# A hybrid decoder step on one core: x loaded in whole rows by token tile, and the first projection begun with half of the tokens

## The chip, the core and the metric

The kernel runs on one core of one Trainium2 chip. The metric is the device time of one execution in microseconds, the median of repeated runs. The engines named below are TensorE (PE in the profile; its weight loads are PEld), VectorE (DVE), ScalarE (ACT), GpSimd (POOL) and SyncE (SP), which issues most of the DMA transfers. Each engine works through its own instructions in their order and stops at a wait until a semaphore has reached a value.

## The reference, cut to what matters

One layer of a decoder over 512 prompt tokens and 8 x 4 sample tokens, 544 in all, with 1024 channels in float32. Only the first lines bear on the change:

```python
def token_mixer(x, w_in, w_out, lb, ...):
    proj = x @ w_in                       # 544 x 1024 @ 1024 x 3584
    q, fz, i, g, gb, gc, cx = jnp.split(proj, ...)
    ...                                   # HGRN2 recurrence, short gated convolution
    return jnp.concatenate([o, yc], axis=-1) @ w_out, S_new, new_buf

def trunk(x, ...):
    m, S_l, b_l = token_mixer(x, ...)
    x = layer_norm(ALPHA * x + m, ln1_g, ln1_b)
    x = layer_norm(ALPHA * x + grouped_moe(x, w_router, ...), ln2_g, ln2_b)
```

Every part that follows (the recurrence, the output projection, the router, 16 experts of width 512) needs the projection, and so does the end of the kernel.

## The kernel before, in words

**Arithmetic.** A float32 matrix product is made of three products of rounded parts: each operand is split into a part `hi` (a copy in the type fp32r) and a rest `lo` (the operand minus `hi`), and hi*hi, hi*lo and lo*hi are added up in one PSUM bank. ACT writes every `hi`, DVE every `lo`, which needs `hi` first.

**Stages.** First the front, on which the change bears: x arrives, is turned (transposed) by PE, split by ACT and DVE, and the first weights are split. Then 14 chunks of the input projection of 256 columns each (`project_first` for chunk 0, `project(o)` for the others), with the gates, the recurrence and the convolution worked in between; the output projection; layer norm and routing; the experts; the final sum. The order on each engine is written out by hand; no scheduler changes it.

**The front before.** There are five token tiles: four of 128 tokens and one of 32. `xT` holds x turned, channels on the partitions, 544 tokens in the free dimension, for each of 8 channel tiles `kt`. The work goes by halves of the channels, `hf` 0 and 1:

- SP (L441 to L447) issues for a half the 512 columns of each of the five token tiles (rows of 2 KB, 256 KB for a tile of 128 tokens), and then half of the weights of chunk 0 (`w0`, rows of 1 KB, 512 KB). After both halves comes chunk 1 of the weights (1 MB), then constants, masks and parameters, chunk 2, and each later chunk when its buffer is free: chunk c waits for `s_lo` at c - 2, since there are three buffers.
- PE (`turn_x`, L1444) waits for a tile's half, turns it in four transposes into one PSUM bank and goes on to the next tile; there are ten such groups, m = 0 to 9, of which m = 4 and 9 are the tile of 32 tokens. Groups 8 and 9 use banks 3 and 4 a second time.
- ACT (L693) copies each turned group from PSUM into `xT[0]` as `hi`, and DVE (L966) writes `lo` into `xT[1]`. Between the two halves ACT and DVE split the first half of `w0` (L703, L977); after the second half of x they split the second half of `w0` (L713, L983 with 1024 columns), then chunk 1 (the same lines with 2048).
- PE then runs `project_first` (L1461): chunk 0 has two tiles of 128 output columns, n = 0 and 1. For each kt and each of the three products it loads one piece of weights for tokens 0 to 271 (L1477) and once more for tokens 272 to 543 (L1478), into two banks; HT is 272. It takes channel tiles 0 to 3 for both n, waits for the second half of the weights, and takes 4 to 7. That is 96 matmuls of 272 tokens.
- `project(1)` (L1504, L1505) needs chunk 1 split (`s_lo` at 2) and the bank of tile 0 emptied by ACT.
- POOL waits for all ten groups of x and for `s_lo` at 2 and then writes 4 MB of zeros to a buffer in DRAM (L574).

Of the kernel before, what the change touches and what calls it, by code (L numbers as in the profile page):

```python
# [34 lines left out]
P = 128  # L35
D = 1024
KT = D // P
SEQ, DB, DS = 512, 8, 4
NS = DB * DS
T = SEQ + NS  # L40
# [75 lines left out]
def build(nc, a):  # L116
    ctx = ExitStack()

    def sem(name):
        return ctx.enter_context(nc.semaphore(name))  # L120

    with ctx:
# [101 lines left out]
        s_x = [sem(f"x_in{i}") for i in range(2 * NTT)]  # L224
# [82 lines left out]
        def x_bank(m):  # L307

            return (0, 1, 2, 3, 4, 5, 6, 7, 3, 4)[m]

        def x_place(m):

            n = P if m % NTT < 4 else NS
            c0 = P if m == 2 * NTT - 1 else 0
            return bank[x_bank(m)][:, c0:c0 + 4 * n]
# [110 lines left out]
        def _(sp):  # L426
# [14 lines left out]
            for hf in range(2):  # L441
                cols, ks = slice(512 * hf, 512 * hf + 512), slice(4 * hf, 4 * hf + 4)
                for tt in range(4):
                    sp.dma_start(xn[:, tt, cols], a["x_prompt"][0, tt * P:(tt + 1) * P, cols]).then_inc(s_x[NTT * hf + tt], 16)
                sp.dma_start(xn[0:NS, 4, cols], a["x_sample"].rearrange("b t n -> (b t) n")[:, cols]).then_inc(s_x[NTT * hf + 4], 16)
                sp.dma_start(raw[0].rearrange("p (k n) -> p k n", k=KT)[:, ks, :], w0[:, ks, :]).then_inc(
                    s_w0 if hf == 0 else s_raw[0], 16)  # L447
# [235 lines left out]
        def _(act):  # L683
# [9 lines left out]
            def x_hi_front(hf):  # L693
                for tt in range(NTT):
                    m = NTT * hf + tt
                    n = P if tt < 4 else NS
                    act.wait_ge(s_xt, m + 1)
                    src = x_place(m).rearrange("p (k t) -> p k t", k=4)
                    nc.scalar.activation(xT[0][:, 4 * hf:4 * hf + 4, tok(tt)], src, ACT.Copy).then_inc(s_xh, 1)

            x_hi_front(0)
            act.wait_ge(s_w0, 16)
            nc.scalar.activation(split[0][0][:, 0:1024], raw[0][:, 0:1024], ACT.Copy).then_inc(s_h0, 1)  # L703
            x_hi_front(1)
# [40 lines left out]
            for o in range(NCH + 1):  # L745
# [5 lines left out]
                hi(o)  # L751
                if o == 4:
                    act.wait_ge(s_abs, 1)
                    link(nc.scalar.activation(ex[0][:, :, :], ex[0][:, :, :], ACT.Exp, scale=-1.0))
                    nc.scalar.activation(ex[0][:, :, :], ex[0][:, :, :], ACT.Ln, bias=1.0).then_inc(s_lnf, 1)
# [197 lines left out]
        def _(dve):  # L953
# [12 lines left out]
            def x_lo_front(hf):  # L966
                for tt in range(NTT):
                    m = NTT * hf + tt
                    n = P if tt < 4 else NS
# [5 lines left out]
            x_lo_front(0)  # L975
            dve.wait_ge(s_h0, 1)
            tt_(split[0][1][:, 0:1024], raw[0][:, 0:1024], f(split[0][0][:, 0:1024]), ALU.subtract).then_inc(s_l0, 1)  # L977
            x_lo_front(1)
# [74 lines left out]
            for o_ in range(NCH + 1):  # L1053
# [5 lines left out]
                lo(o_)  # L1059
                if o_ == 1:  # L1060
                    dve.wait_ge(s_const, 16)
                    dve.wait_ge(s_mask, 16)
                    link(nc.vector.tensor_copy(masks[:, :], fa(E0, LEVELS * P)))
# [378 lines left out]
        def _(pe):  # L1442
            mm, tr = nc.tensor.matmul, nc.tensor.transpose
            def turn_x(hf):  # L1444
                for tt in range(NTT):
                    m = NTT * hf + tt
                    rows = P if tt < 4 else NS
                    pe.wait_ge(s_x[m], 16)
                    if m >= 8:
                        pe.wait_ge(s_xl, m - 4)  # L1450
                    for j in range(4):
                        kt = 4 * hf + j
                        last = tr(x_place(m)[:, j * rows:(j + 1) * rows], xn[0:rows, tt, kt * P:(kt + 1) * P],
                                  ident[0:rows, 0:rows])
                    last.then_inc(s_xt, 1)

            pe.wait_ge(s_id, 16)
            turn_x(0)
            turn_x(1)

            def project_first():  # L1461

                wh, wl = chunk_weights(0, 0), chunk_weights(0, 1)
                pe.wait_ge(s_xl, NTT)
                pe.wait_ge(s_l0, 1)
                for hf in range(2):
                    if hf:
                        pe.wait_ge(s_lo, 1)
                    for n in range(2):
                        if n == 1 and hf == 0:  # L1470
                            pe.wait_ge(s_xl, 2 * NTT)
                        pb, ps = tile_banks(n)
                        for kt in range(4 * hf, 4 * hf + 4):
                            for i, (w_, x_) in enumerate(((wh, 0), (wh, 1), (wl, 0))):
# [433 lines left out]
```

## Time and profile before

| what | us |
|---|---|
| median of 3 runs (lowest, highest) | 698.58 (697.02, 699.57) |
| the profiled execution's own time | 699.09 |
| its span, first to last instruction | 697.3 |
| PE busy | 663.2 (95%) |
| DVE busy | 505.2 (72%) |
| ACT busy | 344.4 (49%) |
| POOL busy | 134.8 (19%) |

The granted TensorE clock is 0.976 of full speed over the span. PE is busy nearly all of the time. Times in the rows count from the start of the span; 1.8 us of the profiled execution's time lie outside the span. The page cuts the span into 40 slices of 17.4 us, so the whole front lies in the first and in half of the second.

### The profile page before, as it was taken

To read this page: it belongs to the slowest core of one execution; us is meant where nothing else is said; L and a number is where in the kernel's file an instruction comes from. 1 tells how busy PE (TensorE), PEld (TensorE's weight loads), DVE (VectorE), ACT (ScalarE), POOL (GpSimd) and SP (SyncE) were. 2 spreads that over 40 slices of the span, in tenths; PEclk is the share of its full clock that TensorE was granted. 3 is DMA by queue.
4 is the path that set the end of the run, shared out by engine and by line. 5 is a ranking of instruction groups with operands and counts; after the bars stand their busy time and mean duration, and the time that the engine had idled before them with its cause. 6 is when DMAs were issued, how large, how long until landed. Compare 5 with 4: busy or idle time off the path is not lost. (4 is left out here: it accounts for less than half of the span.)

```text
span 697.3 us, 9659 instructions
## 1 busy us (share of the span) xinstructions
PE 663.2 (95%) x3847; PEld 559.2 (80%) x3847; DVE 505.2 (72%) x579; ACT 344.4 (49%) x339; POOL 134.8 (19%) x81
## 2 busy tenths in 40 slices
PE   6999999988999999999979999999999999999786
PEld 5999899988997897577857888888888888888531
DVE  4226336798766384758684999999999999999626
ACT  4537412222226141111505777777777777777402
POOL 0001414422131220400020011111111111100055
PEclk9999999999999999999898999999999999999998
DMA  8951111211612105069346999999999999994164
GB/s 285 381 198 62 61 61 62 69 53 61 190 53 85 53 16 193 0 185 410 138 160 274 328 417 419 397 415 409 407 415 411 404 413 406 410 404 173 47 242 158
DMA packets 48689, 162.56 MB, mean 233 GB/s; under 512 B 4294, under 2 KB 23450, under 8 KB 36364
## 3 DMA queue, kind: packets, MB, share of 16 engines
q1 hardware_dynamic: 41756, 136.62, 51.4%
q0 software_dynamic: 6896, 25.43, 9.3%
q8 instruction: 25, 0.41, 0.2%
q14 instruction: 12, 0.10, 0.0%
HBM read 142.61 MB, written 19.44 MB: 232 GB/s over the span
## 5 line engine op out<-in xcount | busy, mean ns | idle before, releaser
L1322 DVE TENSOR_TENSOR RA<-FA,RA 128x2048 fp32r<-128x2048 f32 x93 | 212.9, 2290 | 29.4 <-ACT RA L859 28.7
L859 ACT ACTIVATE RA<-FA 128x2048 fp32r<-128x2048 f32 x93 | 178.9, 1924 | 46.3 <-PE bank L1777 30.6
L1777 PE MATMUL bank<-RA 128*128 128x512 f32 x768 | 186.9, 399 | 2.7 <-DVE RA L1327 2.6
L1777 PEld LDWEIGHTS bank<-RA 128*128 128x128 f32 x768 | 142.9, 191 | 34.6 <-DVE RA L1327 3.5
L1504 PE MATMUL bank<-RA 128*128 128x272 f32 x432 | 110.3, 292 | 0.0
L1505 PE MATMUL bank<-RA 128*128 128x272 f32 x432 | 109.6, 290 | 0.0
L1789 PE MATMUL bank<-RA 128*128 128x512 f32 x384 | 89.9, 390 | 1.4 <-DVE RA L1332 1.4
L1789 PEld LDWEIGHTS bank<-RA 128*128 128x128 f32 x384 | 72.0, 188 | 16.5 <-DVE RA L1332 1.6
L1504 PEld LDWEIGHTS bank<-RA 128*128 128x128 f32 x432 | 82.5, 191 | 0.0
L1505 PEld LDWEIGHTS bank<-RA 128*128 128x128 f32 x432 | 82.3, 191 | 0.0
L983 DVE TENSOR_TENSOR RA<-FA,RA 128x2048 fp32r<-128x2048 f32 (+1 forms) x18 | 48.6, 2700 | 27.3 <-ACT RA L713 27.0
L713 ACT ACTIVATE RA<-FA 128x2048 fp32r<-128x2048 f32 (+1 forms) x18 | 33.6, 1867 | 58.1 <-PE bank L1505 27.5
L1497 PE MATMUL bank<-RA 128*128 128x256 f32 (+1 forms) x480 | 58.8, 282 | 2.0 <-ACT FA L725 2.0
L1497 PEld LDWEIGHTS bank<-RA 128*128 128x128 f32 (+1 forms) x480 | 56.1, 172 | 4.7 <-ACT FA L725 2.4
L629 POOL DMA_INDIRECT FA<-x_by_token,ids x16 | 39.7, 2483 | 79.8 <-DVE ids L1299 60.2
L646 POOL DMA_DIRECT2D y_by_slot<-FA x16 | 9.1, 571 | 236.5 <-DVE FA L1339 236.5
L1659 PE MATMUL bank<-RA 128*128 128x512 f32 x192 | 48.3, 408 | 0.0
L1659 PEld LDWEIGHTS bank<-RA 128*128 128x128 f32 x192 | 36.7, 194 | 10.9 <-issue 2.5
L584 POOL TENSOR_TENSOR FA<-FA 128x1024 f32<-128x1024 f32 (+1 forms) x7 | 16.6, 2365 | 113.5 <-PE bank L1539 69.3
L760 ACT ACTIVATE FA<-FA 128x2048 f32<-128x2048 f32 (+1 forms) x7 | 13.6, 1947 | 49.7 <-POOL FA L585 49.7
L1042 DVE COPY_PREDICATED FA<-masks,bank 128x512 f32<-128x512 uint8 x28 | 20.1, 734 | 22.3 <-PE bank L1539 21.9
L1539 PE MATMUL bank<-FA 128*128 128x128 f32 x256 | 31.0, 278 | 3.9 <-DVE FA L1042 3.9
(237 smaller groups left out, 774.1 us busy)
## 6 DMA issues: line engine op xcount, KB each, us to landing
FA<-w_up SPq DMA_DIRECT2D x32, 1024.0 KB, 7.6
FA<-w_gate SPq DMA_DIRECT2D x32, 1024.0 KB, 7.3
FA<-w_down SPq DMA_DIRECT2D x32, 1024.0 KB, 7.8
FA<-w_in SPq DMA_DIRECT2D x13, 1024.0 KB, 4.9
y_by_slot<-FA POOLq DMA_DIRECT2D x16, 512.0 KB, 7.5
y_by_slot<-FA POOLq DMA_DIRECT2D x1, 4096.0 KB, 18.1
FA<-w_out SPq DMA_DIRECT2D x4, 1024.0 KB, 5.0
FA<-x_prompt SPq DMA_DIRECT2D x8, 256.0 KB, 5.4
```

Source lines behind the costliest of these rows:

```text
L629: pool.indirect_dma_start(out=xg[par], out_offset=None, in_=x1_dram, in_offset=bass.IndirectOffsetOnAxis(ap=ids[:, bi:bi + 1].bitcast(U32) ...
L713: nc.scalar.activation(split[o % 2][0][:, cs], raw[o % 3][:, cs], ACT.Copy).then_inc(s_hi, 1)
L859: nc.scalar.activation(split[split_slot(bi, j)][0], raw[place], ACT.Copy).then_inc(m_hi, 1)
L983: tt_(split[o % 2][1][:, cs], raw[o % 3][:, cs], f(split[o % 2][0][:, cs]), ALU.subtract).then_inc(s_lo, 1)
L1322: tt_(sl[1], raw[place], f(sl[0]), ALU.subtract).then_inc(m_lo, 1)
L1497: last = mm(pb[0:rows, 0:CW], xT[x_][:, kt, tok(j)], w_[:, kt, :], start=(kt == 0 and i == 0), stop=(kt == KT - 1 and i == 2))
L1504: mm(pb[:, 0:HT], lhs, xT[x_][:, kt, 0:HT], start=first, stop=end)
L1505: last = mm(ps[:, 0:HT], lhs, xT[x_][:, kt, HT:T], start=first, stop=end)
L1539: last = mm(bank[4 + p % 3][:, cols], lf[:, h, cols], rf[:, h, cols], start=True, stop=True)
L1659: last = mm(w_bank(half, tt)[0:rows, :], xT[x_][:, k0 + kt, tok(tt)], w_[:, kt, :], start=(conv and kt == 0 and i == 0), stop=(not conv an ...
L1777: last = mm(out[:, :], xgT[par][x_][:, kt, :], w[w_][:, t, :], start=(kt == 0 and i == 0), stop=(kt == KT - 1 and i == 2))
L1789: last = mm(bank[5 + g][:, :], hT[x_][:, kt, :], w[w_][:, t, 512 * g:512 * g + 512], start=(kt == 0 and i == 0), stop=(kt == 3 and i == 2))
```

## The change

x is loaded in whole rows of 4 KB, one transfer for each token tile. The three first tiles come first, then the two halves of `w0`, then tiles 3 and 4. `turn_x(tt)` turns both halves of a tile after one wait. Before the projection PE turns tiles 0 to 2 alone. The projection of chunk 0 is then cut by tokens and no longer by channels: part 0 makes tokens 0 to 271 for n = 0 and n = 1, all eight channel tiles, and part 1 makes tokens 272 to 543 for both. Tile 3 is turned after part 0 of n = 0, tile 4 after part 0 of n = 1. ACT and DVE split tiles 3 and 4 after the second half of `w0` and before chunk 1. The PSUM banks of the turned groups are dealt out anew. The numbers of matmuls, transposes and splits stay.

```diff
         def x_bank(m):
-            return (0, 1, 2, 3, 4, 5, 6, 7, 3, 4)[m]
+            return (4, 5, 6, 7, 2, 3, 4, 5, 6, 7)[m]
...
             w0 = w_in[:, :, ORDER[0][1] * CW:(ORDER[0][1] + 1) * CW]
-            for hf in range(2):
-                cols, ks = slice(512 * hf, 512 * hf + 512), slice(4 * hf, 4 * hf + 4)
-                for tt in range(4):
-                    sp.dma_start(xn[:, tt, cols], a["x_prompt"][0, tt * P:(tt + 1) * P, cols]).then_inc(s_x[NTT * hf + tt], 16)
-                sp.dma_start(xn[0:NS, 4, cols], a["x_sample"].rearrange("b t n -> (b t) n")[:, cols]).then_inc(s_x[NTT * hf + 4], 16)
-                sp.dma_start(raw[0].rearrange("p (k n) -> p k n", k=KT)[:, ks, :], w0[:, ks, :]).then_inc(
-                    s_w0 if hf == 0 else s_raw[0], 16)
+            for tt in range(3):
+                sp.dma_start(xn[:, tt, :], a["x_prompt"][0, tt * P:(tt + 1) * P, :]).then_inc(s_x[tt], 16)
+            for ks, signal in ((slice(0, 4), s_w0), (slice(4, 8), s_raw[0])):
+                sp.dma_start(raw[0].rearrange("p (k n) -> p k n", k=KT)[:, ks, :], w0[:, ks, :]).then_inc(signal, 16)
+            sp.dma_start(xn[:, 3, :], a["x_prompt"][0, 3 * P:4 * P, :]).then_inc(s_x[3], 16)
+            sp.dma_start(xn[0:NS, 4, :], a["x_sample"].rearrange("b t n -> (b t) n")).then_inc(s_x[4], 16)
             load_w(1)
...
-            x_hi_front(0)
+            for tt in range(3):
+                x_hi_front(tt)
             act.wait_ge(s_w0, 16)
             nc.scalar.activation(split[0][0][:, 0:1024], raw[0][:, 0:1024], ACT.Copy).then_inc(s_h0, 1)
-            x_hi_front(1)
...
                 hi(o)
+                if o == 0:
+                    x_hi_front(3)
+                    x_hi_front(4)
...
                 lo(o_)
+                if o_ == 0:
+                    x_lo_front(3)
+                    x_lo_front(4)
...
             pe.wait_ge(s_id, 16)
-            turn_x(0)
-            turn_x(1)
+            for tt in range(3):
+                turn_x(tt)
 
             def project_first():
 
                 wh, wl = chunk_weights(0, 0), chunk_weights(0, 1)
-                pe.wait_ge(s_xl, NTT)
+                pe.wait_ge(s_xl, 6)
                 pe.wait_ge(s_l0, 1)
-                for hf in range(2):
-                    if hf:
-                        pe.wait_ge(s_lo, 1)
+                for part, cols in enumerate((slice(0, HT), slice(HT, T))):
+                    if part:
+                        pe.wait_ge(s_xl, 2 * NTT)
                     for n in range(2):
-                        if n == 1 and hf == 0:
-                            pe.wait_ge(s_xl, 2 * NTT)
-                        pb, ps = tile_banks(n)
-                        for kt in range(4 * hf, 4 * hf + 4):
+                        to = tile_banks(n)[part]
+                        for kt in range(KT):
+                            if n == 0 and kt == 4 and part == 0:
+                                pe.wait_ge(s_lo, 1)
                             for i, (w_, x_) in enumerate(((wh, 0), (wh, 1), (wl, 0))):
-                                first, end = kt == 0 and i == 0, kt == KT - 1 and i == 2
-                                lhs = w_[:, kt, n * P:(n + 1) * P]
-                                mm(pb[:, 0:HT], lhs, xT[x_][:, kt, 0:HT], start=first, stop=end)
-                                last = mm(ps[:, 0:HT], lhs, xT[x_][:, kt, HT:T], start=first, stop=end)
-                        if hf:
+                                last = mm(to[:, 0:HT], w_[:, kt, n * P:(n + 1) * P], xT[x_][:, kt, cols],
+                                          start=(kt == 0 and i == 0), stop=(kt == KT - 1 and i == 2))
+                        if part:
                             last.then_inc(s_tile, 1)
+                        else:
+                            turn_x(3 + n)
```

On PE before, from the last groups turned to the first matmuls of the projection (L1453 are transposes, L1477 and L1478 matmuls; `x_in8` is the semaphore of one tile's half, `xT_lo` counts the groups split by DVE):

```order
L1453 MATMUL bank3<-FA 128x128 [waits xT_lo,x_in8]
L1453 MATMUL bank3<-FA 128x128 x3
L1453 MATMUL bank4<-FA 128x32 [waits xT_lo,x_in9]
L1453 MATMUL bank4<-FA 128x32 x3
L1477 MATMUL bank0<-RA 128x272 [waits lo_first_half,xT_lo]
L1478 MATMUL bank2<-RA 128x272
```

On PE after the change, from tile 2 of x to the start of chunk 1 (L1452 are transposes, L1474 the matmuls of chunk 0):

```order
L1452 MATMUL bank2<-FA 128x128 [waits x_in2]
L1452 MATMUL bank2<-FA 128x128 x3
L1452 MATMUL bank3<-FA 128x128 x4
L1474 MATMUL bank0<-RA 128x272 [waits lo_first_half,xT_lo]
L1474 MATMUL bank0<-RA 128x272 x11
L1474 MATMUL bank0<-RA 128x272 [waits lo_done]
L1474 MATMUL bank0<-RA 128x272 x11
L1452 MATMUL bank4<-FA 128x128 [waits x_in3]
...
L1474 MATMUL bank1<-RA 128x272 x24
L1452 MATMUL bank6<-FA 128x32 [waits x_in4]
...
L1474 MATMUL bank2<-RA 128x272 [waits xT_lo]
L1474 MATMUL bank2<-RA 128x272 x23
```

Eight transposes of 128 tokens and eight of 32, which stood ahead of the projection, now stand in it, and the second half of the matmuls has a wait of its own for `xT_lo`.

On SP before, the first transfers (in const_f32 the identity, then x, the halves of w0, and chunk 1):

```order
L427 DMA FA<-const_f32 128x128
L444 DMA FA<-x_prompt 128x512 x4
L445 DMA FA<-x_sample 32x512
L446 DMA FA<-w_in 128x4x256
L444 DMA FA<-x_prompt 128x512 x4
L445 DMA FA<-x_sample 32x512
L446 DMA FA<-w_in 128x4x256
L438 DMA FA<-w_in 128x8x256
```

On SP after the change, the same stretch:

```order
L425 DMA FA<-const_f32 128x128
L440 DMA FA<-x_prompt 128x1024 x3
L442 DMA FA<-w_in 128x4x256 x2
L443 DMA FA<-x_prompt 128x1024
L444 DMA FA<-x_sample 32x1024
L436 DMA FA<-w_in 128x8x256
```

Ahead of the first half of w0 there are now 1536 KB of x where there were 1088 KB; ahead of the second half 1536 KB where there were 2176 KB.

On ACT after the change, from the last of tile 2 to chunk 1 (L695 splits x, L700 and L709 weights; `raw_in0` and `raw_in1` are the transfers of the second half of w0 and of chunk 1):

```order
L695 ACTIVATE RA<-bank3 128x4x128 [waits x_transposed]
L700 ACTIVATE RA<-FA 128x1024 [waits w0_first_half_in]
L709 ACTIVATE RA<-FA 128x1024 [waits raw_in0]
L695 ACTIVATE RA<-bank4 128x4x128 [waits x_transposed]
L695 ACTIVATE RA<-bank5 128x4x128 [waits x_transposed]
L695 ACTIVATE RA<-bank6 128x4x32 [waits x_transposed]
L695 ACTIVATE RA<-bank7 128x4x32 [waits x_transposed]
L709 ACTIVATE RA<-FA 128x2048 [waits raw_in1]
```

The split of chunk 1 now stands behind the last group of x, which PE turns in the middle of its projection; DVE has the same order.

## Rows read from the trace of the kernel before

**Rows 1.** The page's busy times, the engine with the largest share.

```profile
PE 663.2 (95%) x3847; PEld 559.2 (80%) x3847; DVE 505.2 (72%) x579; ACT 344.4 (49%) x339; POOL 134.8 (19%) x81
```

**Rows 2.** Busy time in stretches: stretch, length, busy of each engine, clock, DMA share, GB/s.

```profile
core 0: us, PE busy (x) PEld busy (x) DVE busy (x) ACT busy (x) POOL busy (x), PEclk, DMA share, GB/s
14.59:26.80 12.21, 12.21 (x99) 12.21 (x98) 4.94 (x5) 5.91 (x9) 1.10 (x1) 1.00 1.08 360
26.80:60.00 33.20, 33.20 (x267) 33.20 (x266) 9.21 (x4) 18.30 (x25) 0.00 (x0) 1.00 0.63 234
```

**Rows 3.** What PE waited for over the span: us in total, times, longest.

```profile
PE bank L1453 <- DMA FA<-x_prompt: 6.5, 3, 4.0
PE bank L1497 <- ACT FA L725: 2.0, 2, 1.6
```

**Rows 4.** Timeline of PE, 3 to 15 us: start, length, engine, line, what, count.

```profile
3.98 1.09 PE L1453 MATMUL bank<-FA 128*128 128x128 f32 x4 [3.98 <-DMA FA<-x_prompt]
5.60 2.97 PE L1453 MATMUL bank<-FA 128*128 128x128 f32 x16 [0.54 <-DMA FA<-x_prompt]
10.53 4.13 PE L1453 MATMUL bank<-FA 128*128 128x128 f32 x20 [1.96 <-DMA FA<-x_prompt]
14.59 0.42 PE L1477 MATMUL bank<-RA 128*128 128x272 f32 x1
```

**Rows 5.** Two DMAs, tile 3's first half and w0's second: issue, time to landing.

```profile
L444 SPq DMA_DIRECT2D FA<-x_prompt x1: 432/432/432, 2.6 to 2.6; - x1
DMA to landing us min/median/max: 4.3/4.3/4.3
...
L446 SPq DMA_DIRECT2D FA<-w_in x1: 425/425/425, 6.7 to 6.7; - x1
DMA to landing us min/median/max: 7.8/7.8/7.8
```

**Rows 6.** Timelines of ACT and DVE in the front, the splits of weights.

```profile
9.85 1.06 ACT L703 ACTIVATE RA<-FA 128x1024 fp32r<-128x1024 f32 x1 [0.84 <-DMA FA<-w_in]
17.48 1.92 ACT L713 ACTIVATE RA<-FA 128x2048 fp32r<-128x2048 f32 x1 [1.56 <-DMA FA<-w_in]
...
10.94 1.23 DVE L977 TENSOR_TENSOR RA<-FA,RA 128x1024 fp32r<-128x1024 f32 x1 [1.17 <-ACT RA L703]
19.44 2.29 DVE L983 TENSOR_TENSOR RA<-FA,RA 128x2048 fp32r<-128x2048 f32 x1 [2.25 <-ACT RA L713]
```

**Rows 7.** Splits of x by form, 4 to 15.9 us: busy us, mean ns of one.

```profile
L699 ACT ACTIVATE RA<-bank 128x512 fp32r<-128x512 f32 x8 | 4.8, 597 | 5.9 <-PE bank L1453 5.8
L699 ACT ACTIVATE RA<-bank 128x128 fp32r<-128x128 f32 x2 | 0.5, 274 | 0.0
...
L972 DVE TENSOR_TENSOR RA<-bank,RA 128x128 fp32r<-128x128 f32 x2 | 0.6, 281 | 0.0
```

**Rows 8.** Busy time in three shorter stretches of the front; columns as in rows 2.

```profile
7.90:8.60 0.70, 0.67 (x7) 0.39 (x5) 0.54 (x2) 0.66 (x2) 0.00 (x0) 1.00 0.93 278
...
10.50:11.20 0.70, 0.67 (x5) 0.44 (x5) 0.26 (x1) 0.41 (x1) 0.00 (x0) 1.00 1.04 397
11.30:14.60 3.30, 3.30 (x17) 2.49 (x17) 2.85 (x4) 2.18 (x4) 0.00 (x0) 0.50 1.10 334
```

**Rows 9.** Transposes: two short pieces of the timeline, and the line's durations.

```profile
5.87 1.27 PE L1453 MATMUL bank<-FA 128*128 128x128 f32 x5
...
10.53 0.66 PE L1453 MATMUL bank<-FA 128*128 128x128 f32 x4 [1.96 <-DMA FA<-x_prompt]
...
L1453 PE MATMUL bank<-FA x40: 221/421/476, 4.0 to 14.4; 128*128 128x128 f32 x32, 32*128 32x32 f32 x8
14.03 0.50 PEld L1453 LDWEIGHTS bank<-FA 32*128 32x128 f32 x4 [0.33 <-issue]
```

**Rows 10.** SP's transfer of chunk 4 of the weights: issue, time to landing.

```profile
L438 SPq DMA_DIRECT2D FA<-w_in x1: 368/368/368, 21.8 to 21.8; - x1
DMA to landing us min/median/max: 14.7/14.7/14.7
```

**Rows 11.** The page's group of token-major matmuls, 24 in a row into one bank.

```profile
L1497 PE MATMUL bank<-RA 128*128 128x256 f32 (+1 forms) x480 | 58.8, 282 | 2.0 <-ACT FA L725 2.0
```

More of the change, by code:

```diff
@@ L223, in build @@
         s_const, s_mask, s_par, s_s0 = sem("const_in"), sem("mask_in"), sem("param_in"), sem("s0_in")
-        s_x = [sem(f"x_in{i}") for i in range(2 * NTT)]
+        s_x = [sem(f"x_in{i}") for i in range(NTT)]
         s_raw = [sem(f"raw_in{i}") for i in range(3)]
@@ L307, in x_bank @@
         def x_bank(m):
-            return (0, 1, 2, 3, 4, 5, 6, 7, 3, 4)[m]
+            return (4, 5, 6, 7, 2, 3, 4, 5, 6, 7)[m]
         def x_place(m):
-            n = P if m % NTT < 4 else NS
-            c0 = P if m == 2 * NTT - 1 else 0
-            return bank[x_bank(m)][:, c0:c0 + 4 * n]
+            return bank[x_bank(m)][:, 0:4 * (P if m < 8 else NS)]
         def sum_banks(tt):
@@ L690, in link, with x_hi_front @@
                 act.wait_ge(s_ac, chain[0])
[L693 to L696, printed above, removed]
+            def x_hi_front(tt):
+                for hf in range(2):
+                    m = 2 * tt + hf
                     act.wait_ge(s_xt, m + 1)
@@ L965, in _, with x_lo_front @@
             link(nc.vector.memset(eps_ln, LN_EPS))
[L966 to L969, printed above, removed]
+            def x_lo_front(tt):
+                for hf in range(2):
+                    m = 2 * tt + hf
                     dve.wait_ge(s_xh, m + 1)
@@ L973, in x_lo_front @@
                         ALU.subtract).then_inc(s_xl, 1)
-            x_lo_front(0)
+            for tt in range(3):
+                x_lo_front(tt)
             dve.wait_ge(s_h0, 1)
             tt_(split[0][1][:, 0:1024], raw[0][:, 0:1024], f(split[0][0][:, 0:1024]), ALU.subtract).then_inc(s_l0, 1)
-            x_lo_front(1)
             def lo(o):
@@ L1443, in _, with turn_x @@
             mm, tr = nc.tensor.matmul, nc.tensor.transpose
[L1444 to L1450, printed above, removed]
+            def turn_x(tt):
+                rows = P if tt < 4 else NS
+                pe.wait_ge(s_x[tt], 16)
+                for hf in range(2):
+                    m = 2 * tt + hf
                     for j in range(4):
@@ L1457, in _ @@
             pe.wait_ge(s_id, 16)
-            turn_x(0)
-            turn_x(1)
+            for tt in range(3):
+                turn_x(tt)
             def project_first():
                 wh, wl = chunk_weights(0, 0), chunk_weights(0, 1)
-                pe.wait_ge(s_xl, NTT)
+                pe.wait_ge(s_xl, 6)
                 pe.wait_ge(s_l0, 1)
-                for hf in range(2):
-                    if hf:
-                        pe.wait_ge(s_lo, 1)
+                for part, cols in enumerate((slice(0, HT), slice(HT, T))):
+                    if part:
+                        pe.wait_ge(s_xl, 2 * NTT)
                     for n in range(2):
-                        if n == 1 and hf == 0:
-                            pe.wait_ge(s_xl, 2 * NTT)
-                        pb, ps = tile_banks(n)
-                        for kt in range(4 * hf, 4 * hf + 4):
+                        to = tile_banks(n)[part]
+                        for kt in range(KT):
+                            if n == 0 and kt == 4 and part == 0:
+                                pe.wait_ge(s_lo, 1)
                             for i, (w_, x_) in enumerate(((wh, 0), (wh, 1), (wl, 0))):
-                                first, end = kt == 0 and i == 0, kt == KT - 1 and i == 2
-                                lhs = w_[:, kt, n * P:(n + 1) * P]
-                                mm(pb[:, 0:HT], lhs, xT[x_][:, kt, 0:HT], start=first, stop=end)
-                                last = mm(ps[:, 0:HT], lhs, xT[x_][:, kt, HT:T], start=first, stop=end)
-                        if hf:
+                                last = mm(to[:, 0:HT], w_[:, kt, n * P:(n + 1) * P], xT[x_][:, kt, cols],
+                                          start=(kt == 0 and i == 0), stop=(kt == KT - 1 and i == 2))
+                        if part:
                             last.then_inc(s_tile, 1)
+                        else:
+                            turn_x(3 + n)
                 pe.wait_ge(s_par, 64)
```

## The prediction

> **What bounds the kernel now.** I read the page's busy times first: PE is busy 95% of the span [rows 1]. Then the busy times by stretch, from the start: from the first matmul of the projection at 14.59 us PE is busy for 12.21 of 12.21 us, and on to 60 us for 33.20 of 33.20 [rows 2]. Then what PE waited for: 6.5 us on transfers of x, and of all later waits the first (2.0 us, on ACT) comes in a stretch whose work is itself released by earlier projection tiles [rows 3]. The reader is to see that behind 14.59 us PE holds everything else. A shift of the end of chunk 0, which now ends as chunk 1 starts at about 26.8, therefore goes one for one into the total, both ways. The question is only when chunk 0 ends.
>
> The timeline of PE in the front [rows 4] shows what comes ahead of it: transposes at 3.98, from 5.60 to 8.57, a gap of 1.96 us, and transposes again from 10.53 to 14.66, as the second halves of x land. In the window 7.9 to 8.6 and again at 10.5 to 11.2 the granted clock is 1.00, but from 11.3 to 14.6, after the gap, it is 0.50 (the level of 1.2 GHz); it is 1.00 again in the projection [rows 8, 2]. So before the change the slow stretch falls upon transposes that wait for data anyway, and the 96 matmuls run at full clock.
>
> **When the projection starts.** The new start needs tile 2 of x turned and split, and the first half of w0 split. I place transfers by the KB ahead of them in the queue, the identity's 64 KB counted.
>
> Before, tile 3's first half (1088 KB with all ahead) was there at 2.6 + 4.3 = 6.9, the first half of w0 (1664 KB) at 9.85, where ACT's wait ended, and the second half of w0 (3264 KB) at 6.7 + 7.8 = 14.5 [rows 5, 6]. That is 195 KB/us from 6.9 to 9.85, and 344 KB/us after that. Tile 0 whole (576 KB) is there at 5.6, where PE's second wait ended with the same bytes moved [rows 4]. Tile 1 (1088 KB) follows at 6.9. Tile 2 (1600 KB) lands between 6.9 + 512/344 = 8.4 and 6.9 + 512/195 = 9.5; I take 9.0. The first half of w0 (2112 KB) lands between 9.9 (8.4 + 1.5) and 9.85 + 448/344 = 11.15; I take 10.6.
>
> A transpose takes a slot of (1.27 - 0.42)/4 = 0.21 us at the start, where 0.42 is the median of one, and at most (0.66 - 0.22)/3 = 0.15 later, when the clock is full, where 0.22 is the shortest; half of 0.21 is the lower bound there [rows 9]. Eight cost 1.7, or 0.9 to 1.2. PE turns tile 0 from 5.6 to 7.3, tile 1 to about 8.6, tile 2 from 9.0 to 10.0, its last result at 10.3. ACT copies the last group, 0.60 [rows 7], to 10.9. Then the first half of w0: 1.06 on ACT to 12.0, 1.23 on DVE [rows 6] to 13.3 with the handovers. The projection starts at 13.3, that is 1.3 us sooner than at 14.59. Bounds: with the early landings 12.6 (2.0 sooner); with the late ones and tile 2 turned at the slow spacing 14.4 (0.2 sooner).
>
> **What the projection now carries.** Its 96 matmuls stay. That 24 in a row go to one bank costs nothing that the trace shows: the token-major tiles do so at 58.8/480 = 0.12 us each [rows 11], and 12.21/99 is 0.12 too [rows 2].
>
> - Tile 3 turned inside: 8 transposes at full clock, 0.9 to 1.2, at most 1.7: I take 1.0. Its transfer (3136 KB) lands at about 14.1 by the same rates, before PE comes to it behind 24 matmuls (3.0 us), so no wait.
> - Tile 4 turned inside: four such loads took 0.50 [rows 9] at the slow clock, so eight cost 0.5 to 1.0: 0.5.
> - The wait for `xT_lo` ahead of part 1. Nothing lies between PE's last transpose and it, so PE stands still for the end of that transpose (0.2 to 0.3), ACT 0.27, DVE 0.28 [rows 7] and three handovers: 0.85, bounds 0.7 to 1.0. Everything is queued behind it, part 1 of both tiles.
> - The wait for the second half of w0 in the middle of the first 24 matmuls costs nothing: it lands near 12.6, ACT is free for it at 12.0 and done at 13.7, DVE takes 1.23 more, to 14.9; PE comes there at 13.3 + 1.5 = 14.8 at full clock, later at half.
> - The clock. PE idles from 10.3 to 13.3, 3.0 us; before, a gap of 1.96 was followed by 3.3 us at 0.50 with PE busy throughout [rows 8]. That stretch now falls on matmuls. 3.3 us at half clock do 1.65 us of work. I take 1.7 lost; from both sides, 0 (the clock stays) and 2.4 (a slow stretch longer by as much as the gap is, half as long again: 3.3 x 1.5 / 2).
>
> The work behind chunk 0 has cover. ACT and DVE split chunk 1 only after tile 4: 1.92 and 2.29 us [rows 6], some 4.1 from the point where part 1 starts, and part 1 runs for 48 slots, 6.0. PE stays covered by 1.9 us; without that cover the rest of it would be paid. Chunk 4 of the weights, whose transfer waits for that split, is issued some 6 us later than 21.8, took 14.7 to land beside POOL's write of zeros [rows 10], and is split only after 50 us, so it stays hidden too. SP issues 11 transfers where it issued 13.
>
> Sum: -1.3 + 1.0 + 0.5 + 0.85 + 1.7 = +2.75 us. The end of chunk 0 goes from 26.8 to about 29.5. The profiled execution's 699.09 would be 701.8; it stands 0.5 above the median of the runs, 698.58, so the median is predicted at 701.3. Ends of the sum: -2.0 + 0.9 + 0.5 + 0.7 + 0 = +0.1 and -0.2 + 1.7 + 1.0 + 1.0 + 2.4 = +5.9.
>
> A rule against part of this. The clock was 1.00 at 7.9 to 8.6 and at 10.5 to 11.2, when PE had run nothing but transposes [rows 8]. The Trainium skill, TensorE: Matmul & The Clock Gate, section Part 4: PE-mode transpose, says that the full clock does not engage for transposes, which do not count as a busy PE in the same way. By that rule tile 2 would be turned at the slow spacing; the trace disagrees, since the spacing of transposes also shrank there.
>
> **The rivals.**
>
> 1. The clock stays full. For it: transposes up to 10.3 leave less room for a gap ahead of a drop; the start may come earlier. Against: the gap is half as long again as the one that a drop followed. Then +1.05: 699.6.
> 2. The transfers bring no earlier start. Whole rows put 448 KB more ahead of the first half of w0, and ACT and DVE must split all of tile 2 ahead of it. For it: the slow 195 KB/us at just this point in the queue. Start at 14.4, tile 3 at 1.0, clock 2.0: -0.2 + 1.0 + 0.5 + 0.85 + 2.0 = +4.2, with the slow spacing +5: 703.2.
> 3. The other side: faster. The start moves by more than the projection takes on. It decides at 1.0 + 0.5 + 0.85 = 2.35 us with the clock full, so at a start before 12.2. That needs tile 2 by 8.0 and the first half of w0 by 9.8, as if rows of 4 KB moved at 400 KB/us and more. A start at 11.4 gives -0.85: 697.7. Against: 344 KB/us is the rate shown, and the split of the weights alone takes 2.3 us behind the last copy.
> 4. Transposes never raise the clock. Tile 2 then costs 0.7 more ahead of the start and nothing else changes, as matmuls run before tile 3: +3.45: 702.0. The spacing of rows 9 speaks against it. It is the result of the skill's rule above.
>
> **How the numbers follow.** The forecast has 0.45, rival 1 0.23, rival 2 0.19, rival 3 0.07, rival 4 0.04; 0.02 is for what I don't see. A measurement of this kernel can tell about 0.5% from no change, here 3.5 us: slower means above 702.1, faster below 695.1. Slower takes most of rival 2 (0.16), half of rival 4 and a third of the forecast, whose own range is 699.8 to 703.2: 0.34. Faster is out of reach of rival 3 (it would need a start before 9, ahead of the first half of w0), so 0.04 for all else. The rest is 0.62. The ends of the sum put the median at 698.7 to 704.5; the runs of the kernel before spread by 1.3 to either side. With most of rival 3 left out at the bottom the range is 697.7 to 705.0.
>
> **What would show it.** In the profile after: the first L1474 starts at 12.6 to 14.4; the clock is 0.50 for some 3 us that overlap it; the matmuls of chunk 0 fall into four blocks with L1452 between them; PE waits once for DVE, 0.7 to 1.0 us, ahead of part 1; L1503 starts at 28.5 to 31; no new wait ahead of L1503. It is wrong if the start is before 12.2, if L1503 waits for the split of chunk 1, or if later stages do not keep the shift.

## The result, and the profile after

| | before | changed |
|---|---|---|
| median (lowest, highest), 14 runs each | 699.09 (695.50, 700.79) | 700.95 (698.15, 703.56) |
| ratio to the kernel before, 95% interval | | 1.0031 [1.0017, 1.0045] |
| profiled execution, span | 699.09, 697.3 | 698.15, 696.3 |
| mean granted clock of the profiled execution | 0.976 | 0.977 |
| first matmul of chunk 0 / chunk 1 | 14.59 / 26.79 | 12.58 / 28.48 |

The change costs 1.9 us in the median, 0.3%: clear of the interval, but under the 0.5% that was called a difference. The profiled execution of the changed kernel happens to be a fast one, faster than that of before. So the times are compared by the medians, and the profile is read where it is sharp: at the two ends of chunk 0.

The timeline of PE from 4 to 12.7 us, which answers to [rows 4], in two rows of transposes and the first matmul:

```profile
4.49 3.65 PE L1452 MATMUL bank<-FA 128*128 128x128 f32 x16 [4.49 <-DMA FA<-x_prompt]
8.30 1.25 PE L1452 MATMUL bank<-FA 128*128 128x128 f32 x8 [0.16 <-DMA FA<-x_prompt]
12.58 0.56 PE L1474 MATMUL bank<-RA 128*128 128x272 f32 x1 [3.03 <-DVE RA L976]
```

The last transpose of tile 2 ends at 9.55, and PE stands for 3.03 us until DVE has made `lo` of the weights. Pieces of the same timeline further on, one for each block change:

```profile
16.99 1.04 PE L1452 MATMUL bank<-FA 128*128 128x128 f32 x8
17.78 0.37 PE L1474 MATMUL bank<-RA 128*128 128x272 f32 x1
...
20.97 0.68 PE L1452 MATMUL bank<-FA 32*128 32x32 f32 x8
22.34 0.39 PE L1474 MATMUL bank<-RA 128*128 128x272 f32 x1 [0.69 <-DVE RA L970]
...
28.45 0.24 PE L1481 MATMUL bank<-FA 84*128 84x84 f32 x1
28.48 0.37 PE L1503 MATMUL bank<-RA 128*128 128x272 f32 x1
```

The start moved by -2.01, chunk 1 by +1.69; chunk 0 takes 15.90 us instead of 12.20. The busy times of the changed kernel by stretch, which answer to [rows 2, 8]:

```profile
core 0: us, PE busy (x) PEld busy (x) DVE busy (x) ACT busy (x) POOL busy (x), PEclk, DMA share, GB/s
28.45:60.00 31.55, 31.55 (x254) 31.55 (x253) 9.21 (x4) 16.62 (x25) 0.00 (x0) 1.00 0.63 233
8.70:9.50 0.80, 0.80 (x8) 0.61 (x6) 0.69 (x1) 0.43 (x2) 0.00 (x0) 1.00 1.12 393
9.60:12.10 2.50, 0.00 (x0) 0.00 (x0) 2.18 (x3) 2.27 (x4) 0.00 (x0) 1.00 1.07 310
12.20:15.40 3.20, 2.82 (x12) 2.85 (x13) 1.46 (x2) 0.26 (x1) 0.00 (x0) 0.50 1.10 325
```

From 12.2 to 15.4 the clock is 0.50, and now it lies on the first matmuls: 12 of them in 2.82 us. After chunk 1 has started PE is busy all the time again. ACT and DVE around the weights (timelines, answering to [rows 6]):

```profile
9.15 1.08 ACT L695 ACTIVATE RA<-bank 128x512 fp32r<-128x512 f32 x2 [0.37 <-PE bank L1452]
10.12 1.06 ACT L700 ACTIVATE RA<-FA 128x1024 fp32r<-128x1024 f32 x1
21.85 1.91 ACT L709 ACTIVATE RA<-FA 128x2048 fp32r<-128x2048 f32 x1
...
11.21 1.23 DVE L976 TENSOR_TENSOR RA<-FA,RA 128x1024 fp32r<-128x1024 f32 x1
23.79 2.29 DVE L981 TENSOR_TENSOR RA<-FA,RA 128x2048 fp32r<-128x2048 f32 x1 [1.51 <-ACT RA L709]
```

ACT goes from the copies of tile 2 to the weights without a wait, so the transfer of the weights, which had landed at 9.8, was not what the start waited for. Chunk 1 is split by 26.1, 2.4 us ahead of its first matmul, more than the 1.9 us of cover that the prediction worked out.

### The profile page after: what moved, and what is told of

Same layout as the page of the kernel before. It is cut to its first block and busy times, and to the rows that moved or that the text cites. A ratio compares the mean times of both kernels' runs of the same rounds, so it can differ in the third digit from the quotient of the medians.

```text
span 696.3 us, 9652 instructions
## 1 busy us (share of the span) xinstructions
PE 662.1 (95%) x3847; PEld 558.1 (80%) x3847; DVE 505.1 (73%) x579; ACT 344.1 (49%) x339; POOL 134.8 (19%) x81
## 5 line engine op out<-in xcount | busy, mean ns | idle before, releaser
L1323 DVE TENSOR_TENSOR RA<-FA,RA 128x2048 fp32r<-128x2048 f32 x93 | 212.9, 2290 | 28.5 <-ACT RA L858 27.8
L1503 PE MATMUL bank<-RA 128*128 128x272 f32 x432 | 109.1, 289 | 0.0
L1504 PE MATMUL bank<-RA 128*128 128x272 f32 x432 | 108.5, 288 | 0.0
L709 ACT ACTIVATE RA<-FA 128x2048 fp32r<-128x2048 f32 (+1 forms) x18 | 33.6, 1867 | 54.0 <-PE bank L1504 26.3
L1658 PEld LDWEIGHTS bank<-RA 128*128 128x128 f32 x192 | 35.5, 188 | 10.5 <-issue 2.5
```

The costliest lines, as they stand in the source:

```text
L709: nc.scalar.activation(split[o % 2][0][:, cs], raw[o % 3][:, cs], ACT.Copy).then_inc(s_hi, 1)
L1323: tt_(sl[1], raw[place], f(sl[0]), ALU.subtract).then_inc(m_lo, 1)
L1658: last = mm(w_bank(half, tt)[0:rows, :], xT[x_][:, k0 + kt, tok(tt)], w_[:, kt, :], start=(conv and kt == 0 and i == 0), stop=(not conv an ...
```

## The experiments

Chunk 1's start and the landings come from one profile for each kernel, the ratios from comparisons with the kernel before on the same chip (10 to 12 executions of the kernel tried).

**The clock: fill the gap.** The changed kernel with matmuls whose result is not used:

```diff
             for tt in range(3):
                 turn_x(tt)
+            pe.wait_ge(s_xh, 3)
+            for _ in range(20):
+                mm(bank[0][:, 0:256], xT[0][:, 0, 0:P], xT[0][:, 1, 0:256], start=True, stop=True)
```

> The changed kernel with 20 matmuls of 256 columns on data that is already there, into bank 0 that the projection clears, put in PE's idle gap ahead of the projection (3.0 us in the changed kernel's profile); their result is not used. Theory A (the slow clock is a term of its own, about 1.5 us, and is caused by that gap): the clock stays 1.00 from about 8.7 on, the projection starts at 12.6 as it did, and chunk 1 begins at 27.0 instead of 28.5; the time is 1.5 us under the changed kernel's, within 0.1% of the kernel before. Rival B (the extra time comes from the new order of the matmuls themselves, 24 in a row into one bank): chunk 1 still begins at 28.5 or later, and the time does not fall.

Ratio 0.9994 [0.9978, 1.0010]. In the timeline of PE and the busy times of this kernel:

```profile
9.89 2.96 PE L1461 MATMUL bank<-RA 128*128 128x256 f32 x20
13.22 0.36 PE L1477 MATMUL bank<-RA 128*128 128x272 f32 x1 [0.37 <-DVE RA L976]
27.81 0.37 PE L1506 MATMUL bank<-RA 128*128 128x272 f32 x1
...
13.30:27.70 14.40, 13.71 (x112) 13.45 (x113) 5.57 (x7) 6.07 (x10) 1.09 (x1) 1.00 0.85 283
```

The clock is 1.00 all through chunk 0, which takes 14.59 us (27.81 - 13.22) instead of 15.90: the slow stretch cost 1.3. Rival B, the order of the matmuls, fails. Chunk 1 begins at 27.8 and not at 27.0, since tile 0 landed later in this execution (PE began at 4.88, not 4.49) and the clock first rose at 10.7, when the unused matmuls already ran (8.7 in the changed kernel), so that tile 2 was turned at the slow spacing; the start is again 2.99 us behind the last transpose, at 10.23. It is the length of chunk 0 that a single profile can tell, not the place of its start.

**The wait: turn tile 4 with tile 3.**

```diff
-                        else:
-                            turn_x(3 + n)
+                        elif n == 0:
+                            turn_x(3)
+                            turn_x(4)
```

> The changed kernel with tile 4 turned right behind tile 3, after part 0 of n = 0; part 0 of n = 1 then stands between the last transpose and the wait of part 1. Theory A (the wait ahead of part 1 costs its 0.7 us because nothing lies between): no wait there any more, chunk 1 begins 0.7 us earlier, at 27.8, with the clock as in the changed kernel. x_sample landed at 14.1 and PE comes to it at about 17.5, so no new wait. Rival: PE waits the same 0.7 elsewhere (for ACT or DVE, for the transfer of tile 4, or for chunk 1, whose split would now be further ahead), and chunk 1 begins at 28.5.

Ratio 1.0008 [0.9991, 1.0025]. What PE waited for from 12 to 60 us, first in this kernel, then in the changed one:

```profile
PE bank L1474 <- DVE RA L976: 3.0, 1, 3.0
```

```profile
PE bank L1474 <- DVE RA L976: 3.0, 1, 3.0
PE bank L1474 <- DVE RA L970: 0.7, 1, 0.7
```

The wait of 0.7 is gone and none has come in its place. Chunk 0 runs from 13.00 to 28.21, 15.21 us: 0.69 less than 15.90. The length of chunk 0 fell as theory A has it, and the rival fails. Chunk 1 itself began at 28.2 and not at 27.8, for a start that was 0.42 later in this execution.

**Turn everything first.** All five tiles ahead of the projection, the loads and the cut by tokens kept:

```diff
-            for tt in range(3):
+            for tt in range(NTT):
+                if tt == 3:
+                    pe.wait_ge(s_xl, 4)
                 turn_x(tt)
...
                         if part:
                             last.then_inc(s_tile, 1)
-                        else:
-                            turn_x(3 + n)
```

> The changed kernel with all five tiles turned ahead of the projection; loads and the cut by tokens stay as in the changed kernel. Theory A (turning inside the projection gives back what the early start brings): the start waits for x_sample, which landed at 14.1, and comes at 14.6 to 15.0; nothing is turned inside and nothing waits, so chunk 1 begins at 26.9 to 27.3 if the clock is full, up to 28.5 if the slow stretch falls on the matmuls. Rival B (the cut by tokens is what costs): the 96 matmuls take over 12.5 us at full clock. Rival C (the early start is worth its whole 2.0 us): chunk 1 begins 2 us later than in the changed kernel, at 30.5.

Ratio 1.0035 [1.0015, 1.0055]. The busy times of this kernel, and the timeline's first matmuls of chunks 0 and 1:

```profile
12.40:15.10 2.70, 2.70 (x16) 2.37 (x16) 2.04 (x4) 1.40 (x3) 0.00 (x0) 0.50 1.12 355
15.20:19.10 3.90, 3.90 (x18) 3.90 (x18) 2.26 (x4) 2.19 (x2) 0.00 (x0) 0.50 1.03 372
19.30:29.00 9.70, 9.70 (x80) 9.70 (x79) 1.18 (x2) 2.66 (x5) 1.09 (x1) 1.00 1.08 371
...
15.18 0.59 PE L1476 MATMUL bank<-RA 128*128 128x272 f32 x1
29.14 0.37 PE L1503 MATMUL bank<-RA 128*128 128x272 f32 x1
```

The start came near the place given (15.2 for 14.6 to 15.0), but not for the reason given: x_sample landed at 12.9 in this execution and not at 14.1, and PE turned without a further wait from 12.33 on, tile 3 at the slow spacing of 0.21 us. The end was missed: 29.1 lies beyond the 28.5 given. The slow stretch was twice as long, from 12.4 to 19.2, and four microseconds of it lay on matmuls. Without it the matmuls take what they took before: 80 in 9.70 us is 0.12 each, so rival B, a cost of the cut by tokens, fails here too. Rival C expected chunk 1 at 30.5 and fails by 1.4. Whether turning early or late is better does not come out clean. With the clock's cost on the matmuls taken off (2.0 of 13.96 us) this order would have ended chunk 0 at 27.1, the changed kernel (1.3 off) at 27.2; but here the slow stretch lay on the transposes ahead of the start too, and tiles 3 and 4 had landed over 1 us sooner. The ratios, 1.0035 and 1.0031, show no gain of the early start over waiting for all of x, and do not decide theory A either.

**Both edits together.**

> The changed kernel with both edits: the 20 unused matmuls in the gap, and tile 4 turned with tile 3. If the terms add (theory A): chunk 1 begins at 28.5 - 1.5 - 0.7 = 26.3, 0.5 us ahead of the kernel before, a time 0.1% under it, which this measurement hardly tells from no change. If they overlap (the rival), it begins at 27.0 as with the matmuls in the gap alone.

Ratio 0.9991 [0.9970, 1.0012]. Chunk 0 from 12.84 to 26.71:

```profile
26.71 0.37 PE L1507 MATMUL bank<-RA 128*128 128x272 f32 x1
12.90:26.60 13.70, 13.70 (x112) 13.49 (x113) 5.50 (x7) 5.88 (x10) 1.09 (x1) 1.00 1.09 352
```

13.87 us: less by 2.03 than 15.90, and 1.31 + 0.69 is 2.00. The terms add. The clock had risen at 8.9, ahead of the gap, and stayed at 1.00, so this is also the cleaner proof that the filled gap keeps it. The end is 26.7, not 26.3, for the start, 0.26 later, and a slow stretch that was worth 1.3 and not 1.5.

**The kernel before, its gap filled.** The same idea in the kernel before, 14 matmuls between the halves of x:

```diff
             turn_x(0)
+            pe.wait_ge(s_xl, 2)
+            for _ in range(14):
+                mm(bank[0][:, 0:256], xT[0][:, 0, 0:P], xT[0][:, 1, 0:256], start=True, stop=True)
             turn_x(1)
```

> The kernel before with 14 unused matmuls of 256 columns in its own gap (8.6 to 10.5 us), ahead of the second halves of x. Theory A (the clock falls because of the gap, in the kernel before too, where the slow stretch hits only transposes that wait for data one by one): the clock stays 1.00, the last tile is turned at 13.6 to 13.9 instead of 14.6, chunk 1 begins 0.6 to 1.0 us earlier than at 26.8. Rival (the transposes there are bound by the transfers): chunk 1 begins at 26.6 to 26.8, no change.

Ratio 0.9966 [0.9945, 0.9986]. Timeline and busy times:

```profile
8.56 1.93 PE L1461 MATMUL bank<-RA 128*128 128x256 f32 x14
10.33 1.36 PE L1453 MATMUL bank<-FA 128*128 128x128 f32 x8
11.95 1.75 PE L1453 MATMUL bank<-FA 128*128 128x128 f32 x12 [0.26 <-DMA FA<-x_prompt]
13.62 0.39 PE L1480 MATMUL bank<-RA 128*128 128x272 f32 x1
25.78 0.37 PE L1507 MATMUL bank<-RA 128*128 128x272 f32 x1
...
10.50:13.60 3.10, 2.71 (x20) 1.81 (x19) 2.53 (x4) 2.03 (x4) 0.00 (x0) 1.00 1.09 344
```

The stretch behind the gap, at 0.50 in [rows 8], has the clock at 1.00. The projection starts 0.97 sooner and chunk 1 1.01 sooner; the second halves of x landed 0.1 to 0.3 sooner in this execution, which can be a part of it. So the gap caused the slow stretch in the kernel before as well, and it was not free there: the prediction called it hidden behind the transfers, and 0.7 us (the last run below, where the transfers were no earlier than before) to 1 us of it was not.

**Rows of 2 KB again.** The changed kernel, tiles 0 to 2 each by two transfers (and `turn_x` waits for both):

```diff
             for tt in range(3):
-                sp.dma_start(xn[:, tt, :], a["x_prompt"][0, tt * P:(tt + 1) * P, :]).then_inc(s_x[tt], 16)
+                for hc in (slice(0, 512), slice(512, 1024)):
+                    sp.dma_start(xn[:, tt, hc], a["x_prompt"][0, tt * P:(tt + 1) * P, hc]).then_inc(s_x[tt], 16)
```

> The changed kernel with each of the tiles 0 to 2 of x loaded by two transfers of rows of 2 KB (256 KB each) instead of one of 4 KB rows, in the same order. In the changed kernel tile 0 landed at 4.4, tile 2 at 8.25 and the first half of w0 at 9.8, all earlier than predicted from the kernel before (5.6, 9.0, 10.6). If whole rows are what makes the transfers faster: tile 0 lands at 5.2 or later, w0's first half at 10.5 or later and the projection starts 0.5 us or more after 12.6. If not (the order alone, or the variation from run to run, in which w0's first half landed between 9.0 and 10.0 in four profiles): tile 0 at 4.4 to 4.9, w0's first half at 9.0 to 10.0, and the start still 3.0 us behind the last transpose of tile 2.

One profile. First the issue and landing of tile 1's second half and of w0's first half, then the timeline of PE:

```profile
L441 SPq DMA_DIRECT2D FA<-x_prompt x1: 433/433/433, 2.6 to 2.6; - x1
DMA to landing us min/median/max: 5.4/5.4/5.4
...
L443 SPq DMA_DIRECT2D FA<-w_in x1: 433/433/433, 4.0 to 4.0; - x1
DMA to landing us min/median/max: 6.8/6.8/6.8
...
4.87 1.94 PE L1453 MATMUL bank<-FA 128*128 128x128 f32 x8 [4.87 <-DMA FA<-x_prompt]
8.03 3.68 PE L1453 MATMUL bank<-FA 128*128 128x128 f32 x16 [1.22 <-DMA FA<-x_prompt]
14.69 0.57 PE L1475 MATMUL bank<-RA 128*128 128x272 f32 x1 [2.98 <-DVE RA L977]
```

And in the changed kernel the landing of tile 1 whole, and of w0's first half:

```profile
L440 SPq DMA_DIRECT2D FA<-x_prompt x1: 424/424/424, 1.7 to 1.7; - x1
DMA to landing us min/median/max: 4.4/4.4/4.4
...
L442 SPq DMA_DIRECT2D FA<-w_in x1: 433/433/433, 2.6 to 2.6; - x1
DMA to landing us min/median/max: 7.2/7.2/7.2
```

Tile 1, the first 1088 KB of the queue, is complete at 8.0 with half rows and at 6.1 with whole ones; the weights at 10.8 and 9.8. Two of the three signs of "whole rows are faster" are there (w0 after 10.5, start over 0.5 us later, at 14.69 for 12.58); tile 0 landed within 0.4 us of the same time. In three profiles of the order of before, with rows of 2 KB, the same 1088 KB had landed at 6.9 to 7.0; in eight with whole rows tile 1 was there at 5.9 to 6.3. A single profile can't price it, and it does not separate the length of the rows from the number of transfers: each issue holds SP for 0.4 us or more, so with half rows tile 1 is complete only with the issue of 2.6 instead of 1.7, and w0 is issued at 4.0 instead of 2.6. Before the change the last of these bytes were also issued at 2.6, and took 4.3 us to land [rows 5], no longer than tile 1's 4.4 with whole rows. Part of the late start is the clock as well: all 16 transposes of the second row above run at the slow spacing, (3.68 - 0.42)/15 = 0.22, and the matmuls behind them stay at 0.23 each until 17.5. The start is once more 2.98 behind the last transpose.

**The changed kernel once more.**

> The changed kernel as it is, a second profile. If the 1.7 us that its first profile lost at chunk 1 and had back by the output projection (198 us) came back by a slow stretch of the clock that the kernel before happened to have there (151 to 155 us) and it had not, then where this profile has a slow stretch between 27 and 240 us it is later there, and where it has none it is not; chunk 1 begins at 28.1 to 28.9. If later stages absorb the shift in itself, it is back at the time of the kernel before (updates at 243.8) with or without such a stretch.

Chunk 0 runs from 12.46 to 28.39. No slow stretch fell between 27 and 240 us, as in the first profile, and the first state update came at 243.68. This run alone could not decide; the next paragraph takes all profiles together.

**Where 1.7 us went back.** In the first pair of profiles the changed kernel is 1.69 behind at chunk 1 and level at the first state update (L1593 before, L1592 after): 243.76 and 243.80. Busy times from 151.3 to 154.5 us, before and after:

```profile
151.30:154.50 3.20, 3.20 (x17) 3.20 (x16) 2.85 (x3) 0.00 (x0) 2.49 (x2) 0.50 0.00 0
```

```profile
151.30:154.50 3.20, 2.42 (x20) 2.42 (x21) 3.14 (x7) 0.00 (x0) 1.18 (x1) 1.00 0.00 0
```

The kernel before ran these at 0.50, the changed one at 1.00. The time from chunk 1's first matmul to the first state update, in all 12 profiles:

```
slow stretch near 151 or 168 us   before 216.97, tiles 3 and 4 together 216.84, both edits 216.81,
                                  before with its gap filled 216.85 and 216.80
none between 27 and 240 us        changed 215.32 and 215.29, gap filled 215.34, all first 215.31,
                                  half rows 215.29, the two versions below 215.37 and 215.32
```

There are two values and nothing between. So the later stages absorb nothing: a shift of chunk 1 arrives whole, to a tenth, whether it is -1.0 or +3.8 us. What came back is one slow stretch of the clock, 1.5 to 1.6 us. In the kernel before it follows a wait of PE of 1.95 us that ends at 150.49, and the changed kernel has the same wait, to 152.08, without the stretch: in some executions it comes, in others not. Another stands at 294.6 to 297.9 in the profile of before alone (0.50 against 1.00), so the two profiled totals can't show the 1.69.

**A version to beat both.** Tiles 3 and 4 turned together, the first half of w0 loaded and split ahead of tile 2, unused matmuls around tile 2. Of the edit only PE's part ahead of the projection is shown; `hold_clock(n)` issues n of the unused matmuls:

```diff
-            for tt in range(3):
-                turn_x(tt)
+            turn_x(0)
+            turn_x(1)
+            pe.wait_ge(s_xh, 3)
+            hold_clock(8)
+            turn_x(2)
+            hold_clock(11)
```

> A version meant to beat both: the changed kernel with tiles 3 and 4 turned together, the first half of w0 loaded and split ahead of tile 2 (the second half behind tile 2), and 8 and 11 unused matmuls in the gaps around tile 2's transposes. Theory A (the start lies 3.0 us behind the last transpose of tile 2 because ACT's copy, then ACT's and DVE's split of the weights follow it): now only the copy and DVE's lo of tile 2 follow, 1.5 us, tile 2 lands 1.5 us later, at 9.8; start at 12.2 to 12.5, chunk 1 at 26.0 to 26.4, 0.4 to 0.8 us ahead of the kernel before, some 0.1% in time. Rival: the start waits for the second tile's order (DVE busy with the weights) or for w0's second half in the middle of the first block, and chunk 1 begins at 26.7 or later, as with both edits alone.

Ratio 0.9982 [0.9961, 1.0003], chunk 0 from 12.90 to 26.77, level with the kernel before. The start was expected at 12.2 to 12.5. PE's timeline shows why:

```profile
8.35 2.07 PE L1461 MATMUL bank<-RA 128*128 128x256 f32 x8
10.22 1.10 PE L1454 MATMUL bank<-FA 128*128 128x128 f32 x8
```

Tile 2 had landed at 8.9, but the unused matmuls ran at the slow spacing and held PE until 10.2. They were then left out, and 7 stood behind tile 2:

> The version meant to beat both, mended: its 8 unused matmuls ahead of tile 2 ran at the slow spacing (0.21 us, from 8.35 to 10.2) and held back tile 2, which had landed at 8.9. They are left out, and 7 instead of 11 stand behind tile 2. Theory A (start = last transpose of tile 2 and 1.6 us): last transpose at about 9.9, start at 11.4 to 11.7, chunk 1 at 25.3 to 25.6 if the clock is full from the start, 1.2 us ahead of the kernel before and 0.2 to 0.4 ahead of the kernel before with its gap filled; up to 26.9 if the slow stretch falls on the matmuls. Rival: DVE is still at the weights' lo until 11.4, or w0's second half (split after tile 2) comes too late in the first block, and chunk 1 begins at 26.5 or later even at full clock.

Ratio 1.0000 [0.9983, 1.0016], chunk 0 from 12.80 to 26.99:

```profile
9.42 1.97 PE L1454 MATMUL bank<-FA 128*128 128x128 f32 x8 [0.75 <-DMA FA<-x_prompt]
11.04 1.84 PE L1461 MATMUL bank<-RA 128*128 128x256 f32 x7
12.80 0.59 PE L1483 MATMUL bank<-RA 128*128 128x272 f32 x1
...
11.43 1.32 DVE L971 TENSOR_TENSOR RA<-bank,RA 128x512 fp32r<-128x512 f32 x2
```

Wrong again, by 1.1 us or more at the start. Tile 2 landed 0.5 later, and its transposes all ran at the slow spacing (last end 11.39 for 9.9). The chain behind them was as expected: DVE ends `lo` of tile 2 at 12.75 and the projection starts at 12.80, 1.41 behind the last transpose where 1.6 was given. PE's timeline shows no wait only because the 7 unused matmuls, at the slow spacing too, last just as long; the start could not have come sooner without them. Chunk 1 at 26.99 lies where the rival had it, but of its two causes neither is seen: PE stands neither for the weights' `lo` nor in the first block. Here PE's clock was low until 13.5, and this version has nothing that raises it sooner.

**The best one again.**

> The kernel before with the 14 unused matmuls in its gap, once more, on the chip of the mended version: chunk 1 at 25.6 to 25.9 and a time 0.15 to 0.4% under the kernel before, if the 0.34% (interval 0.14 to 0.55) of its first run was not chance. The part that the front gives is 1.05 us, 0.15%; what lies above that would be the clock's lottery later on.

Ratio 0.9976 [0.9958, 0.9994]; chunk 1's first matmul at 26.10, 0.69 sooner than before, a little later than the 25.6 to 25.9 given; the second halves of x landed 0.3 to 0.4 later than in its first run, and no sooner than in the kernel before. Both comparisons of this kernel lie clear below 1, by 0.34% and 0.24%, as no other version's does; it is the kernel before with 14 matmuls more. The 0.7 to 1.0 us at chunk 1 are 0.10 to 0.14%; where the rest comes from is not shown. Nor is it told apart from the version meant to beat both in its first form (0.9982), whose median was 698.05 where this kernel's first run had 698.11, on the same chip.

## Why the prediction was right

The predicted 701.3 stands against 700.95, +2.75 us against +1.86 in the medians and +1.69 at chunk 1. The mechanism was the forecast's, and the sign of every term. The sizes were worse than the total makes them look. The two largest errors, the start (0.7) and the clock (0.4), point the same way, and the shift at chunk 1 was forecast 1.06 us too large. That the time came within 0.35 us is partly luck: it was added to a median of 698.58 from 3 runs, and 14 runs put the kernel before at 699.09, 0.5 higher.

| term | predicted | bounds | measured | from |
|---|---|---|---|---|
| start | -1.3 | -2.0, -0.2 | -2.01 | first matmul of chunk 0 |
| tile 3 turned inside | +1.0 | 0.9, 1.7 | +0.79 | 16.99 to 17.78 |
| tile 4 turned inside | +0.5 | 0.5, 1.0 | +0.68 | 22.34 - 20.97 - 0.69 |
| wait ahead of part 1 | +0.85 | 0.7, 1.0 | +0.69 | PE's wait; its removal gave 0.69 |
| clock | +1.7 | 0, 2.4 | +1.31 | length of chunk 0 with the gap filled |
| rest | 0 | | +0.23 | see below |
| sum | +2.75 | +0.1, +5.9 | +1.69 | |

The rest lies for the most part in the matmuls themselves: in the changed kernel with its gap filled the blocks of chunk 0 take 3.09 + 3.19 + 6.12 = 12.40 us against 12.20 before. Tile 3 came out under its lower bound of 0.9, the start and the wait a hundredth outside theirs.

The step of the start was mis-sized. It placed tile 2 at 9.0 and the weights at 10.6; they landed at 8.25 and 9.8, the second just before the early bound of 9.9. The bytes in the queue were counted rightly, but the rates (195 and 344 KB/us) were those of rows of 2 KB and 1 KB with an issue for every 256 KB of x. The issues were counted wrongly: SP issues 8 transfers up to chunk 1 where it issued 13, not 11, and w0's first half at 2.6 us where it was at 3.6. The run with half rows lands later from tile 1 on, but whether the longer rows or the fewer and earlier issues bring the data sooner stays open. The chain behind the last transpose, by contrast, was worked out as 3.0 us and measured 3.03, 3.04, 2.99, 3.04, 3.03 and 2.98 in six profiles. Since that chain follows PE and not the transfers, tile 2's last transpose sets the start.

The slow stretch came where it was put, on the first matmuls, with the gap of 3.03 us ahead of it that was given as 3.0. That a gap causes it is shown from both sides, by filling it in either kernel: in the five profiles in which the clock had risen ahead of an unfilled gap it fell to 0.50 in it or behind it, and in the four with 20 or 14 unused matmuls there it stayed at 1.00 through chunk 0. Rival 1 (the clock stays) is what the filled kernel does, with a start 1.37 sooner than before the change, and its chunk 1, at 27.8, is 1.0 us behind the kernel before, as that rival's +1.05 had it. Rival 2 (no earlier start) did not happen. Rival 3's threshold (a start before 12.2 at full clock) stayed out of reach by 0.4 us even with the early landings. Rival 4 fell by the spacing: the eight transposes of tile 2 take 1.25 us from start to end at 1.00, (1.25 - 0.27)/7 = 0.14 each with 0.27 for the last. The Trainium skill's sentence in TensorE: Matmul & The Clock Gate, section Part 4: PE-mode transpose, that the full clock does not engage for transposes, is not what this trace shows: the clock rose at 8.7, with nothing but transposes ahead of 9.6 us. It rose among transposes in eight of the twelve profiles; in the other four (the changed kernel with only its gap filled, the one with half rows, and the two versions meant to beat both) it rose only after matmuls had begun, and in three of these, all but the first of the two versions, all 24 transposes ahead of the projection had the slow spacing.

One argument of the prediction was wrong though it cost nothing in the sum: that before the change the slow stretch fell on transposes that wait for data anyway. 0.7 to 1 us of it did not, as the two runs of the filled kernel before show.

## What to carry to other kernels

Starting a stage early with part of its data is paid for in the same engine's queue: what stood ahead of the start moves into the stage, and a new dependence inside it can cost a full round over the other engines unless work lies between (0.7 us here, gone once one block of matmuls stood there). Before an idle gap on TensorE is called harmless, look at what runs behind it: the slow clock that it brings on falls on whatever comes next, and some matmuls on data at hand can be cheaper than the gap, if they are not so many that they delay the work they protect. And where two kernels differ by less than a slow stretch of the clock (1.5 us here, come or gone by chance), compare fixed points of the timelines with the stretches beside them, and medians of many executions, not two profiled totals.

## What the runs showed of the hardware

- The spread of a kernel's executions (695.5 to 700.8 for the kernel before) goes in the main with the granted clock: of the 14 of the changed kernel, the three slowest (702.62 to 703.56) had a mean clock of 0.970, the fastest (698.15) 0.977; but one of 701.28 had 0.978.
- At the very start PE's transposes have the slow spacing, 0.21 us, with no low clock in the busy-time rows, which show 1.00 there: ahead of the first rise the spacing tells the clock, and the rows do not. Where the rise comes varies with the execution: near 7.9 in the kernel before, near 8.7 in the changed one, at about 10.7 with its gap filled, 13.5 in the last version and 17.5 with half rows.
- Transfers of the same order land up to 1 us apart from one execution to the next (w0's first half at 9.0 to 10.0 in the changed order), while the same chain of engine work repeats to 0.06 us.
